# Decoder step on one core: accumulating weight transfers held back behind the memory value units, and new instruction orders for the stage

## The reference

```
cross = cross_attend(qm, mk, mv)          # 4 memory heads, 256 memory rows; prompt
cross = cross_attend(qm, cache_mem_k[l], cache_mem_v[l])   # the same for the sampled rows
mix   = concat([mla_out, pool_out, cross]) * silu(gate)
y     = rms_norm(x + mix @ w_out, final_norm)
```

## Time and profile before

| | |
|---|---|
| median of three runs | 879.98 us |
| profiled execution | 879.45 us |
| its span, first to last instruction | 877.8 us |
| PE busy | 98% of the span |
| DVE, ACT, POOL busy | 67%, 53%, 17% |
| memory traffic | 191 GB/s over the span |

### The profile page before, as it was taken

The page is one execution under the profiler, slowest core; times in us unless marked ns, Lnnn a source line. Parts: engine busy times, 40 slices in busy tenths (PEclk is TensorE's granted clock), DMA queues, the critical chain, the costliest instruction groups (busy, mean ns, idle before and its releaser), DMA issues. The chain is left out here.

```text
span 877.8 us, 15782 instructions
## 1 busy us (share of the span) xinstructions
PE 864.2 (98%) x5505; PEld 790.9 (90%) x5505; DVE 591.0 (67%) x1021; ACT 463.9 (53%) x773; POOL 146.2 (17%) x210
## 2 busy tenths in 40 slices
PE   9999999999999999999999999999999899999996
PEld 9999999999999999999999999888887688888885
DVE  6545635442258578888888875966669699564777
ACT  7555432122143466676667654577777455363446
POOL 0003001512300112323232331000001011111113
PEclk9999999999999999999999999999999999999999
DMA  9695535223284487888887762524137667988586
GB/s 354 247 345 172 168 125 178 72 94 103 83 310 144 137 282 233 251 257 253 252 254 245 243 245 67 203 84 157 37 117 236 200 141 189 263 198 261 118 150 215
DMA packets 64878, 168.56 MB, mean 192 GB/s; under 512 B 9672, under 2 KB 27657, under 8 KB 62808
## 3 DMA queue, kind: packets, MB, share of 16 engines
q1 hardware_dynamic: 52528, 126.48, 42.0%
q0 software_dynamic: 10752, 33.56, 16.7%
q10 hardware_dynamic: 1520, 7.51, 2.4%
HBM read 156.14 MB, written 11.50 MB: 191 GB/s over the span
## 5 line engine op out<-in xcount | busy, mean ns | idle before, releaser
L67 PE MATMUL z<-x_hi,w_hi 128*128 128x288 f32 x512 | 152.4, 298 | 0.0
L69 PE MATMUL z<-x_hi,w_lo 128*128 128x288 f32 x512 | 150.8, 295 | 0.0
L68 PE MATMUL z<-x_lo,w_hi 128*128 128x288 f32 x512 | 150.8, 294 | 0.0
L184 ACT ACTIVATE w_hi<-w_raw 128x1024 fp32r<-128x1024 f32 (+2 forms) x62 | 64.8, 1046 | 141.2 <-PE z L69 58.5
L191 DVE TENSOR_TENSOR w_lo<-w_raw,w_hi 128x1024 fp32r<-128x1024 f32 (+2 forms) x62 | 77.3, 1247 | 70.0 <-ACT w_hi L184 69.7
L1002 POOL DMA_DIRECT2D v_raw<-in_cache x128 | 69.2, 540 | 179.6 <-issue 179.6
L67 PEld LDWEIGHTS z<-x_hi,w_hi 128*128 128x128 f32 x512 | 96.1, 188 | 1.7 <-issue 0.2
L68 PEld LDWEIGHTS z<-x_lo,w_hi 128*128 128x128 f32 x512 | 96.1, 188 | 1.7 <-issue 0.2
L69 PEld LDWEIGHTS z<-x_hi,w_lo 128*128 128x128 f32 x512 | 96.0, 188 | 0.0
L2013 ACT ACTIVATE o_hi<-o_raw 128x1024 fp32r<-128x1024 f32 x50 | 52.9, 1059 | 75.1 <-PE pa_s L2980 37.5
L2260 DVE TENSOR_TENSOR o_lo<-o_raw,o_hi 128x1024 fp32r<-128x1024 f32 x50 | 61.0, 1221 | 36.5 <-ACT o_hi L2013 36.5
(11 more groups left out here) (550 smaller groups left out, 2407.6 us busy)
## 6 DMA issues: line engine op xcount, KB each, us to landing
w_raw<-in_w_feat SPq DMA_DIRECT2D x56, 512.0 KB, 3.8
k_raw<-in_cache SPq DMA_DIRECT2D x128, 192.0 KB, 3.0
v_raw<-in_cache POOLq DMA_DIRECT2D x128, 128.0 KB, 3.3
o_raw<-in_w_out POOLq DMA_DIRECT2D x30, 512.0 KB, 8.5
o_raw<-in_w_out SPq DMA_DIRECT2D x20, 512.0 KB, 10.6
w_raw<-in_w_mem_kv SPq DMA_DIRECT2D x16, 512.0 KB, 3.7
gate_spill<-gate_tmp SPq DMA_DIRECT2D x16, 288.0 KB, 3.5
mix<-gate_spill SPq DMA_DIRECT2D x4, 1152.0 KB, 9.8
```

Source lines behind the costliest of these rows:

```text
L67: pe.matmul(out, a[0], b[0], start=start, stop=False, skip_group_check=onto)
L68: pe.matmul(out, a[0], b[1], start=False, stop=False, skip_group_check=onto)
L69: return pe.matmul(out, a[1], b[0], start=False, stop=stop, skip_group_check=onto)
L184: act.activation(hi_slot(s, u)[:, lo:w], s.wraw[:, u % RAW, lo:w], ACT.Copy).then_inc(s.w_hi, 1)
```

## The change

POOL waits, ahead of its first accumulating transfer, for the landing of the second four value units. The written-out lists of ACT, DVE and PE are put in another order; every call of before is still there once. On PE two calls that stood after one another may be separated, and the `used` count moves to the call that ends a unit. The diff, cut:

```diff
@@ gpsimd
                 pool.memset(qp[:], 0.0).then_inc(q_zero, 1)
+                pool.wait_ge(u_in[3], 64)
                 for n in range(2):
...
@@ scalar
-                exps(LASTH, 0)
-                g_queries(0)
-                exps(LASTH, 1)
-                g_queries(1)
                 act.wait_ge(zeroed, 1)
                 piece_high(0)
+                piece_high(1)
+                exps(LASTH, 0)
+                exps(LASTH, 1)
+                exps(LASTH, 2)
+                g_queries(0)
...
                 m_exps(1)
+                out_high(0)
+                g_exps()
                 m_exps(2)
                 m_turned(0, 0)
                 m_turned(0, 1)
+                out_high(1)
+                out_high(2)
+                m_turned(1, 0)
+                g_turned()
+                m_turned(1, 1)
+                m_exps(3)
                 piece_high(2)
...
                 piece_high(3)
-                out_high(2)
-                g_turned()
+                out_high(3)
                 m_turned(2, 0)
+                g_sums(0)
+                m_turned(2, 1)
                 for k in range(0, 8):
                     sample_high(k)
-                g_sums(0)
-                out_high(3)
-                m_turned(2, 1)
+                m_turned(3, 0)
+                piece_high(4)
+                g_sums(1)
                 out_high(4)
-                piece_high(4)
-                m_turned(3, 0)
                 for k in range(8, 12):
                     sample_high(k)
                 m_turned(3, 1)
-                g_sums(1)
                 out_high(5)
                 piece_high(5)
...
@@ vector
                 mix_sum(4)
-                out_low(7)
-                partial(0)
-                piece_low(6)
-                out_low(8)
+                mix_sum(5)
                 out_low(9)
+                piece_low(7)
                 out_low(10)
+                add(0, Q1)
                 out_low(11)
-                mix_sum(5)
-                add(0, Q1)
-                piece_low(7)
                 mix_sum(6)
...
@@ tensor
                 turn(LASTH, 0)
                 turn(LASTH, 1)
+                m_score(2)
+                turn(LASTH, 2)
                 g_scores(1)
-                turn(LASTH, 2)
-                m_score(2)
+                values(LASTH)
                 m_turn(0, 0)
                 m_turn(0, 1)
-                values(LASTH)
                 m_score(3)
+                g_turn()
                 pe.wait_ge(zeroed, 1)
                 out_split(0)
                 y_tile(0, 0)
                 y_tile(0, 1)
+                m_turn(1, 0)
                 m_value(0, 0)
...
                 y_tile(1, 1)
+                g_values(0)
                 m_value(1, 0)
                 m_turn(2, 0)
...
                 y_tile(2, 0)
+                m_value(1, 1)
+                m_turn(2, 1)
+                g_out(0)
+                m_turn(3, 0)
+                y_tile(2, 1)
                 m_value(2, 0)
-                g_out(0)
+                g_values(1)
+                m_value(2, 1)
                 y_sample(0).then_inc(used, 1)
+                g_out(1)
+                m_turn(3, 1)
                 y_sample(1).then_inc(used, 1)
...
                 y_tile(9, 1)
-                y_sample(8).then_inc(used, 1)
-                y_sample(9).then_inc(used, 1)
                 out_split(10)
                 y_tile(10, 0)
-                y_sample(10)
-                y_tile(10, 1).then_inc(used, 1)
+                y_sample(8).then_inc(used, 1)
+                y_tile(10, 1)
+                y_sample(9).then_inc(used, 1)
```

More of the change, by code:

```diff
@@ L2156, in _ @@
                 m_turned(3, 1)
-                g_sums(1)
                 out_high(5)
                 piece_high(5)
-                partial_low(0)
+                out_high(6)
                 for k in range(12, 16):
                     sample_high(k)
-                out_high(6)
+                out_high(7)
                 attention_over(act)
                 piece_high(6)
+                partial_low(0)
+                out_high(8)
                 piece_high(7)
-                out_high(7)
-                out_high(8)
                 piece_high(8)
@@ L2547, in _ @@
                         m_values()
+                dve.wait_ge(zeroed, 1)
+                gate(LASTH - 2)
+                piece_low(0)
                 maxima(LASTH, 0)
@@ L2562, in _ @@
                 gate(LASTH - 1)
-                m_divide(0)
                 turned(LASTH, 0)
                 turned(LASTH, 1)
+                m_divide(0)
+                turned(LASTH, 2)
                 g_maxima()
-                turned(LASTH, 2)
                 m_maxima(2)
+                g_divide()
                 out_low(0)
                 m_divide(1)
-                piece_low(1)
                 m_turned(0, 0)
                 gate(LASTH)
+                out_low(1)
+                m_turned(0, 1)
+                m_divide(2)
                 m_maxima(3)
-                m_turned(0, 1)
-                g_divide()
-                out_low(1)
                 m_gate(0)
                 m_turned(1, 0)
-                m_divide(2)
+                out_low(2)
+                piece_low(2)
                 m_turned(1, 1)
-                piece_low(2)
-                out_low(2)
+                m_divide(3)
                 m_turned(2, 0)
+                out_low(3)
                 m_gate(1)
+                g_gate(0)
+                piece_low(3)
+                m_turned(2, 1)
                 for k in range(0, 8):
                     sample_low(k)
[L2588 to L2591, removed]
+                m_turned(3, 0)
+                piece_low(4)
                 m_gate(2)
-                m_turned(3, 0)
-                piece_low(3)
+                g_gate(1)
                 out_low(4)
+                m_turned(3, 1)
                 for k in range(8, 12):
                     sample_low(k)
-                m_turned(3, 1)
-                g_gate(1)
-                piece_low(4)
+                m_gate(3)
+                out_low(5)
                 attention_over(dve)
@@ L2604, in _ @@
                 mix_sum(1)
-                m_gate(3)
-                out_low(5)
                 piece_low(5)
                 mix_sum(2)
+                out_low(6)
                 for k in range(12, 16):
                     sample_low(k)
+                out_low(7)
                 dve.wait_ge(mixed, 1 + NH + MH)
                 mix_sum(3)
-                out_low(6)
+                out_low(8)
+                piece_low(6)
+                partial(0)
                 mix_sum(4)
-                out_low(7)
-                partial(0)
-                piece_low(6)
-                out_low(8)
+                mix_sum(5)
                 out_low(9)
+                piece_low(7)
                 out_low(10)
+                add(0, Q1)
                 out_low(11)
-                mix_sum(5)
-                add(0, Q1)
-                piece_low(7)
                 mix_sum(6)
+                out_low(12)
                 piece_low(8)
-                out_low(12)
+                out_low(13)
                 mix_sum(7)
-                out_low(13)
                 piece_low(9)
@@ L3051, in _ @@
                 y_tile(0, 1)
+                m_turn(1, 0)
                 m_value(0, 0)
[L3053 to L3056, removed]
                 out_split(1)
                 y_tile(1, 0)
+                m_turn(1, 1)
+                m_value(0, 1)
                 y_tile(1, 1)
+                g_values(0)
                 m_value(1, 0)
                 m_turn(2, 0)
-                m_turn(2, 1)
-                m_value(1, 1)
-                g_values(0)
                 out_split(2)
                 y_tile(2, 0)
+                m_value(1, 1)
[3 more added lines that the diff above has]
+                y_tile(2, 1)
                 m_value(2, 0)
-                g_out(0)
+                g_values(1)
+                m_value(2, 1)
                 y_sample(0).then_inc(used, 1)
+                g_out(1)
+                m_turn(3, 1)
                 y_sample(1).then_inc(used, 1)
[L3071 to L3077, removed]
                 out_split(3)
                 y_tile(3, 0)
+                y_tile(3, 1)
+                m_value(3, 0)
                 m_value(3, 1)
-                y_tile(3, 1)
                 y_sample(2).then_inc(used, 1)
@@ L3084, in _ @@
                 y_tile(4, 0)
+                y_tile(4, 1)
                 y_sample(3).then_inc(used, 1)
-                y_tile(4, 1)
-                y_sample(4).then_inc(used, 1)
                 out_split(5)
                 y_tile(5, 0)
-                y_sample(5)
-                y_tile(5, 1).then_inc(used, 1)
+                y_tile(5, 1)
+                y_sample(4).then_inc(used, 1)
+                y_sample(5).then_inc(used, 1)
                 out_split(6)
@@ L3096, in _ @@
                 y_tile(7, 0)
```

(5 more changed lines are left out.)

13 lines of the change are left out of this document (2 added, 11 removed).

## The result

The changed kernel took 876.22 us (median of 6 runs, 875.44 to 876.76), the kernel before in the same set 880.72 (6 runs): a ratio of 0.9942, 95% interval 0.9929 to 0.9955. Repeated in a later set it took 877.30 against 880.44, 0.9959 (0.9946 to 0.9972); its 11 runs together have a median of 876.67.

A forecast was written before the change was run, and what follows sets the result against it. TensorE was taken as the bound, with two stalls from a shared DMA load. The sum −1.04 − 1.76 + 0.3 + 0.2 − 0.3 = −2.6, or −3.1 without the additions, was taken as −2.8: 877.1 us, range 876.4 to 879.1.

The forecast's parts named there:

- Both stalls: TensorE waits of 1.04 us before the second sample group's value products and 1.76 us after the last matmul of `y_tile(2, 1)`.
- Step 1: POOL's new wait holds accumulating transfers back, so the value units land by 679.1 and the 1.04 us stall goes.
- landings stay as they were: Bound from the other side on the value units: the last lands at 686.6 and 1.9 us are lost.
- Step 2: On ACT, `m_turned(3, 0)` goes ahead of `out_high(4)`, so the 1.76 us stall goes.
- the wait doesn't bring the units earlier: Rival: the value units' queue stays slow, `g_values(1)` stalls 1.9 us, gain only 0.9, 879.1 us; chance 0.07.
- Step 3: TensorE's new list: 0.3 us added at `y_tile(0, 0)`, 0.2 added by more separate transposes, 0.3 gained from two small waits.
- changes of kind: On TensorE, a matmul after a transpose starts 0.31 instead of 0.23 us later; two more such cases add 0.2 us.
- short waits: Two small TensorE waits, at the last `m_value` and at `g_turn`, go; 0.3 us gained.
- Step 4: Other moved ACT and DVE work costs nothing, covered by TensorE's own work; thinnest covers 0.6 to 1.4 us.
- hand-offs: Rival: TensorE's new list alternates work with thin covers; three slips of 0.4 us give back 1.2, 878.4 us; chance 0.16.
- Q3's loads: Rival: SP's loads near 711 us delay accumulating transfers of units 13 to 15; 878.0 to 884.1 us; chance 0.08.
- the step from the stretch to the median: The -2.8 us taken from the profiled 879.45 gives 876.6; the median of three runs, 0.5 higher, makes it 877.1.

The follow-up runs named there:

- e3: The changed kernel without POOL's new wait, so only the reordered lists; 877.88 us, ratio 0.9966 to the kernel before.
- e2: The kernel before plus only POOL's new wait for the value units, all lists in the old order; 876.04 us, ratio 0.9945 to the kernel before.
- e4: The kernel before with one ACT call moved, `m_turned(3, 0)` ahead of `out_high(4)` and `piece_high(4)`; 880.41 us, ratio 0.9996 to the kernel before.

## Why the prediction was right or wrong

- *The place and the origin were right.* Both stalls went, TensorE is full up to the end, and the sum over the changed part, -2.8 with -3.1 as its far end, measured -3.09.
- *Step 1, the landing, was right and understated.* The last value unit landed 9.6 us after its issue (within 12 was asked), POOL's first transfer went out at 677.85 (near 679). The bound "landings stay as they were" is out. The "17.3 against 4.0" said of mixed stretches compares the last of eight units with the first; against the 9.6 of the last unit now, the mixing cost 7.7.
- *Step 2's reason was enough, but not needed.* It credited the 1.76 us to ACT's new order, and e3, with the order and without the wait, has no wait for `pt_lo`. But e2 loses that stall in the old order: unit 4 lands after 10.1 us (10.4 in the changed kernel) instead of 18.6, so ACT is no longer held. The step took unit 4's landing as given ("even a landing at 689.2, that of before") though step 1 itself put it by 682. The one call that it names is not enough alone: e4 keeps a stall of 2.3, as `g_sums(1)` still stands behind `out_high(4)`.
- *The rival "the wait doesn't bring the units earlier"* gave 0.9 us to the lists alone. Its condition didn't come true with the wait, but e3 is that case: the last value unit lands 17.3 us after its issue, and the stretch gains 0.90, 223.89 to 222.99.
- *Step 3's 0.3 at the first `y_tile`* is the 0.30 for ACT's `probs`. The changes of kind (+0.2) and short waits (-0.3) I did not separate: e2, with none of the lists, is 3.29 shorter where the two stalls make 2.80, so 0.5 us more went with them.
- *Step 4's covers held*: nothing else stands in TensorE's list of waits. Neither hand-offs nor Q3's loads bit: SP's loads went out at 710.00, the accumulating transfers issued behind them took 9.2 to 11.1 us but overlapped, the last landing near 727, and unit 14 began at 730.46, 3.91 earlier than in the earlier trace rows, 0.8 of it from the earlier start.
- *What failed is the step from the stretch to the median*, "the median of the three runs is 0.5 higher, 879.98, hence 877.1". It carried the -2.8 over one for one; in the first set the median fell by 4.50 where the profiled stretch fell by 3.09. The step put at nothing what the old stalls cost by the clock in some executions, some 0.3 us on average, which the earlier trace rows, at 1.00, could not show, and it took the time outside the stretch as fixed: in profiles of these kernels `q_pad` starts anywhere from 644.4 to 648.3. The cause of the last 0.6 to 0.8 us stays open. With the same stretch, 220.80 and 220.79, the first set's median was 876.22 and the repetition's 877.30, so on which side of the range's end a set came was in part luck. The range, 0.7 us below the forecast, was too narrow for that.

## What to carry to other kernels

Ask of a late load what else uses the same DMA engines before reordering the engines that wait for it: one wait on the queue that isn't urgent gave the whole gain, and more than eighty moved lines added nothing to it. Price a stall as its gap plus what the clock may do behind it, and compare profiles over a stretch that begins behind the kernel's scattered start; a change of a few us deserves a second set of runs.

## What the runs showed of the hardware

- A transfer that adds into memory on the chip held the DMA engines twice as long per byte as a copy (12.4 against 24.9 GB/s per engine; 194 against 421 GB/s with one queue alone), and slowed the loads of another queue, whose last value unit landed after 17.3 us instead of 11.5, without moving many more bytes (1.33 against 1.22 MB). The Trainium skill (DMA: Bandwidth & Descriptors, Queues, rings and completion order) lets the queues of an engine take turns packet by packet; the trace agrees: from 672 to 675 us the two queues sent 108 and 102 packets, and the adding ones took 74.5% of the time against 32.0%.
- Behind a gap of TensorE of 2.30 us the clock fell to 0.50 in one profile; behind 1.6, 1.8 and 2.7 it did not in others; behind 3.93 it was 0.66 over 5 us in the profile, and the mean clock of all 12 runs was at most 0.996, where with the gap filled all 12 had at least 0.997. A fall cost 1.65 to 1.7 us here. A gap of 2.35 near the kernel's start went with 0.57 over the next 4 us.
